# Expert visits ordered by early counts, gate and up columns split into even and odd, down tiles of the even rows first

## The reference

```
idx, gw = grouped_route(h, w_router, router_bias)      # 2 experts per token, weights sum to 1
order = argsort(idx.reshape(n_assign))                 # slots of one expert lie together
hb  = silu(xb @ w_gate[e]) * (xb @ w_up[e])            # 2048 -> 512
out = hb @ w_down[e]                                   # 512 -> 2048
y[token] += out * gw
x = x + g2 * y ;  return rms_norm(x, final_norm_w)
```

## Time and profile before

| | us |
|---|---|
| median of three runs | 2713.9 |
| profiled execution | 2711.68 |
| its span, first to last instruction | 2709.9 |
| TensorE busy | 2538.5 |
| first gate/up matmul of the expert loop | 1519.55 |
| last hidden transposes | 2681.22 |

### The profile page before, as it was taken

One profiled execution on the slowest core, in us unless ns is written; L12 is line 12 of the kernel. 1 busy time (PEld: TensorE's weight loads), 2 busy tenths in 40 slices (PEclk: granted clock), 3 DMA queues, 4 the chain that ended last, 5 costly groups with the idle time before them and its releaser, 6 DMA issues.

```text
span 2709.9 us, 30984 instructions
## 1 busy us (share of the span) xinstructions
PE 2538.5 (94%) x11966; PEld 1522.0 (56%) x11966; DVE 1302.8 (48%) x1559; ACT 640.4 (24%) x897; POOL 296.5 (11%) x505
## 2 busy tenths in 40 slices
PE   4999999999999987999998799999999898998897
PEld 3577888888768766777886333333333333333332
DVE  4379999999785777544334322222122121211124
ACT  4122222222212285323333111111111011110113
POOL 0000000000121111010001111111111111111111
PEclk8999999999999989999998899999999899999999
DMA  9933333333586572855636999899939999699997
GB/s 336 314 121 101 100 108 101 101 108 101 165 284 205 181 234 78 286 170 155 231 109 252 419 409 410 346 398 404 415 105 407 408 408 377 248 415 406 411 355 297
DMA packets 234063, 710.20 MB, mean 262 GB/s; under 512 B 26290, under 2 KB 120642, under 8 KB 186424
## 3 DMA queue, kind: packets, MB, share of 16 engines
q1 hardware_dynamic: 186624, 555.56, 53.0%
q0 software_dynamic: 37344, 125.58, 14.7%
q10 hardware_dynamic: 9998, 27.71, 2.8%
HBM read 657.60 MB, written 69.81 MB: 268 GB/s over the span
## 4 chain that ended last, share of the span: by engine, by line
PE 38%; DMA 19%; DVE 2%; issue 0%; ACT 0%; SPq 0%; POOL 0%; ACTq 0%; DVEq 0%; POOLq 0%
DMA ring<-in_w_down_dram 17%; PE ps L1739 16%; PE ps L1753 8%; PE ps L1961 4%; PE ps L1963 3%; PE ps L1962 3%; DMA wraw_o<-in_w_out_dram 2%; PE ps L1762 1%; PE ps L1679 1%; DVE tmp L2234 0%; PE ps L1771 0%; DVE hidT L2581 0%; DVE ring L2602 0%; DMA xrow<-h_d,tix 0%; PE ps L1976 0%
## 5 line engine op out<-in xcount | busy, mean ns | idle before, releaser
L1739 PE MATMUL ps<-ring,xT 128*64 128x512 f32 x3136 | 700.6, 604 | 39.6 <-DMA ring<-in_w_up_dram 38.2
L1739 PEld LDWEIGHTS ps<-ring,xT 128*64 128x64 f32 x3136 | 231.7, 139 | 500.7 <-issue 495.9
L1753 PE MATMUL ps<-ring,hidT 128*64 128x512 f32 x1568 | 348.8, 596 | 12.8 <-DMA ring<-in_w_down_dram 5.4
L2576 DVE TENSOR_TENSOR hb<-ps,gsl 128x256 f32<-128x256 f32 x49 | 20.8, 424 | 668.6 <-ACT gsl L2185 668.6
L763 PE MATMUL ps<-hh,wih 128*128 128x512 f32 x1056 | 330.7, 394 | 6.4 <-DVE wil L751 6.4
L763 PE MATMUL ps<-hh,wil 128*128 128x512 f32 x1056 | 331.2, 394 | 0.0
L763 PE MATMUL ps<-hl,wih 128*128 128x512 f32 x1056 | 329.4, 393 | 0.0
L1135 DVE SCALAR_TENSOR_TENSOR acc<-u,vcur,acc 128x1024 f32<-128x1024 f32 x240 | 308.2, 1284 | 7.8
L1753 PEld LDWEIGHTS ps<-ring,hidT 128*64 128x64 f32 x1568 | 107.6, 137 | 220.2 <-issue 191.3
L763 PEld LDWEIGHTS ps<-hh,wih 128*128 128x128 f32 x1056 | 198.9, 189 | 54.5 <-DVE wil L751 7.2
L763 PEld LDWEIGHTS ps<-hl,wih 128*128 128x128 f32 x1056 | 199.2, 189 | 44.4
(11 more groups left out here) (409 smaller groups left out, 3036.3 us busy)
## 6 DMA issues: line engine op xcount, KB each, us to landing
ring<-in_w_gate_dram SPq DMA_DIRECT2D x128, 1024.0 KB, 28.5
ring<-in_w_up_dram SPq DMA_DIRECT2D x128, 1024.0 KB, 30.6
ring<-in_w_down_dram SPq DMA_DIRECT2D x64, 2048.0 KB, 30.3
wm<-in_w_mod_dram POOLq DMA_DIRECT2D x88, 512.0 KB, 4.1
wraw_i<-in_w_in_dram SPq DMA_DIRECT2D x72, 512.0 KB, 3.8
wraw_o<-in_w_out_dram SPq DMA_DIRECT2D x128, 256.0 KB, 3.8
wmA<-in_w_mod_dram SPq DMA_DIRECT2D x32, 512.0 KB, 8.3
u<-in_w_mod_dram POOLq DMA_DIRECT2D x24, 512.0 KB, 4.7
```

The lines of the kernel that those rows point to most:

```text
L1739: last = pe.matmul(ps[BLK * a:BLK * a + BLK, BANK_GU:BANK_GU + FE], xT[:, t, h, :], ring[:, s:s + 2, c0:c0 + FE // 2], start=(q + k == 0), ...
L1753: last = pe.matmul(ps[BLK * a:BLK * a + BLK, BANK_D + 512 * n:BANK_D + 512 * n + 512], hidT[:, t, h, :], ring[:, slot(o, 8 + d), c0:c0 + 512],
```

## The change

Three things are changed.

1. `visit` is now a value that SP loads from DRAM for each expert. In the projection stage, VectorE counts how often the first 512 tokens chose each expert (a new TensorE matmul against ones at piece HALF + 54), ranks the experts (`rank_experts`), puts the ranks on the 32 places (`place_experts`) and stores the order. The router jobs of the first half move some pieces earlier for that. A place is 4 * step, plus 0 or 2 by bit 3 of the rank, plus 1 for the lower half, with step = (3 * (rank mod 8) + 3) mod 8. Block sums in visits order then come from products with two 32 x 32 matrices, `before` (visited earlier) and `at_visit`.
2. `gate_up` runs each quarter first for the even (r = 0) and then for the odd hidden columns (r = 1), with a column step of 2, into two PSUM banks. silu, product, transpose and copy are done per r, with a semaphore `s_gua` when the even ones are complete.
3. `down` takes the tiles 0, 2, 1, 3: both tiles of the even rows, then those of the odd rows.

```
-            def visit(o):
-                return o % G * EG + o // G
+            def visit(eng, o):
+                return eng.value_load(order_d[0:1, o:o + 1], min_val=0, max_val=E - 1)
...
-                        for k in range(4):
-                            h, t = k_tile(q, k)
-                            for a in range(2):
-                                c0 = FE * k + FE // 2 * a
-                                last = pe.matmul(ps[BLK * a:BLK * a + BLK, BANK_GU:BANK_GU + FE], xT[:, t, h, :],
-                                                 ring[:, s:s + 2, c0:c0 + FE // 2], start=(q + k == 0), stop=(q + k == 6))
+                        for r in range(2):
+                            for k in range(4):
+                                h, t = k_tile(q, k)
+                                for a in range(2):
+                                    c0 = FE * k + FE // 2 * a
+                                    last = pe.matmul(ps[BLK * a:BLK * a + BLK, BANK_GU[r]:BANK_GU[r] + FE // 2], xT[:, t, h, :],
+                                                     ring[:, s:s + 2, c0 + r:c0 + FE // 2:2], start=(q + k == 0), stop=(q + k == 6))
+                            if q == 3 and r == 0:
+                                last.then_inc(s_gua, 1)
                         last.then_inc(s_guq[q], 1)
...
-                    for d in range(FT):
-                        h, t = d // 2, d % 2
+                    for d in (0, 2, 1, 3):
+                        a_in, r = d // 2, d % 2
...
+                    sp.wait_ge(s_tab, 1)
+                    sp.dma_start(order_d[:, :], order_w[0:1, :]).then_inc(s_its, 16)
+                    sp.wait_ge(s_its, 16)
+                    experts = [visit(sp, o) for o in range(2)]
                     sp.wait_ge(s_wou, PIECES)
...
                     for r in range(NSLOT, NP * E):
+                        if r % NP == 0:
+                            expert = visit(sp, r // NP)
                         released(r - NSLOT)
...
+                        if g == HALF + 54:
+                            pe.wait_ge(s_ab, 1)
+                            pe.matmul(ps[:, BANK_EC:BANK_EC + HT * E], ones[:], oab[:].rearrange("p j e -> p (j e)"),
+                                      start=True, stop=True).then_inc(s_pre, 1)
...
                             gate_up(pe, j, o)
+                            transpose_hidden(pe, j, 0)
                             pe.wait_ge(s_xs, j + 2)
                             transpose_rows(pe, range(7))
-                            transpose_hidden(pe, j)
+                            transpose_hidden(pe, j, 1)
                             transpose_rows(pe, range(7, 8))
...
-                        act.wait_ge(s_guq[3], i + 1)
-                        act.activation(gsl[:], ps[:, BANK_GU:BANK_GU + FE // 2], ACT.Silu).then_inc(s_gs, 1)
+                        for r in range(2):
+                            act.wait_ge(s_gua if r == 0 else s_guq[3], i + 1)
+                            act.activation(gsl[:, P * r:P * r + P], ps[:, BANK_GU[r]:BANK_GU[r] + P], ACT.Silu).then_inc(s_gs, 1)
...
+                    def rank_experts():
+                        dve.wait_ge(s_pre, 1)
+                        red(ecnt[:], ps[:, BANK_EC:BANK_EC + HT * E].rearrange("p (j e) -> p e j", e=E), ALU.add)
+                        order(dve.scalar_tensor_tensor(out=key[:], in0=ecnt[:], scalar=float(2 * E), in1=wE[:], op0=ALU.mult, op1=ALU.add))
+                        tt(pairs[:], key[:, None, :].broadcast_to((P, E, E)), key[:, :, None].broadcast_to((P, E, E)), ALU.is_gt)
...
+                        if g == HALF + 57:
+                            rank_experts()
+                        if g == HALF + 58:
+                            place_experts()
...
-                    order(dve.tensor_copy(runs(nb[:]), visits(nb_i[:])))
-                    order(dve.tensor_tensor_scan(out=xinc[:], data0=ones[:, 0:E], data1=nb[:], initial=0.0,
-                                                 op0=ALU.mult, op1=ALU.add))
-                    tt(first[:], xinc[:], nb[:], ALU.subtract)
-                    ts(visits(code[:]), runs(first[:]), float(BLK), None, ALU.mult)
+                    ts(nb[:], nb_i[:], float(BLK), None, ALU.mult)
+                    dve.wait_ge(s_g2, 1)
+                    tt(sums[:], before[:], nb[:, None, :].broadcast_to((P, E, E)), ALU.mult)
+                    red(code[:], sums[:], ALU.add)
...
+                    tt(first[:], code[:], nb[:], ALU.add)
+                    tt(sums[:], at_visit[:], first[:, None, :].broadcast_to((P, E, E)), ALU.mult)
+                    red(xinc[:], sums[:], ALU.add)
+                    ts(xinc[:], xinc[:], 1.0 / BLK, None, ALU.mult)
```

More of the change, by code:

```diff
@@ L1480, in xt_piece @@
             def xt_piece(j):
[L1482 removed]
+                return HALF + 14 + 5 * j
             def landing(t):
@@ L1527, in slot, with load @@
                 return SLOT[(NP * o + m) % NSLOT]
-            def load(sp, o, m):
+            def load(sp, o, m, expert):
                 q, kind = m // 2, m % 2
+                e = ds(expert, 1)
                 s = slot(o, m)
@@ L1607, in hybrid_layer @@
             early = choice_tiles(0)
+            assert place_at[0] <= 68 * KB
+            place_at[0] = 68 * KB
+            oab = t3("oab", HT, E)
+            ecnt, key, rank = (t3(n, E) for n in ("ecnt", "key", "rank"))
+            rank_i, step_i = place("rank_i", [P, E], I32), place("step_i", [P, E], I32)
+            bits_i, bits = place("bits_i", [P, 2, E], I32), t3("bits", 2, E)
+            order_w = place("order_w", [P, E], I32)
             assert place_at[0] <= 72 * KB
+            at_visit, before = place("at_visit", [P, E, E], F32, 80 * KB), place("before", [P, E, E], F32, 84 * KB)
+            pairs, sums = place("pairs", [P, E, E], F32, 90 * KB), place("sums", [P, E, E], F32, 72 * KB)
             place_at[0] = xT_at
@@ L1764, in transpose_rows, with transpose_hidden @@
                             last.then_inc(s_xt2, 1)
-                def transpose_hidden(pe, j):
-                    pe.wait_ge(s_hb, j + 1)
-                    v = hb[:].rearrange("p (c t) -> p t c", t=2)
-                    for t in range(2):
-                        pe.transpose(ps[:, BANK_H + 512 * t:BANK_H + 512 * t + P], v[:, t, :], ident[:]).then_inc(s_hbt, 1)
+                def transpose_hidden(pe, j, r):
+                    pe.wait_ge(s_hb, 2 * j + r + 1)
+                    pe.transpose(ps[:, BANK_H + 512 * r:BANK_H + 512 * r + P], hb[:, P * r:P * r + P], ident[:]).then_inc(s_hbt, 1)
                 @block.sync
@@ L1812, in _ @@
                     for m in range(2, 6):
-                        load(sp, 1, m)
+                        load(sp, 1, m, experts[1])
                     sp.wait_ge(s_tbl, 1)
@@ L1816, in _ @@
                     for m in range(6, 9):
-                        load(sp, 1, m)
-                    sp.wait_ge(s_its, 16)
+                        load(sp, 1, m, experts[1])
+                    sp.wait_ge(s_its, 32)
                     n = item_before_last(sp)
@@ L1828, in released @@
                             sp.wait_ge(s_guq[m // 2], blocks_through(words, o))
+                    expert = experts[1]
                     for r in range(NSLOT, NP * E):
+                        if r % NP == 0:
+                            expert = visit(sp, r // NP)
                         released(r - NSLOT)
                         if r % NP < 8:
-                            load(sp, r // NP, r % NP)
+                            load(sp, r // NP, r % NP, expert)
                         elif r % 2 == 1:
-                            load(sp, r // NP, r % NP - 1)
+                            load(sp, r // NP, r % NP - 1, expert)
                     sp.wait_ge(s_dt[FT - 1], blocks_through(words, E - 2))
```

133 lines of the change are left out of this document (82 added, 51 removed).

## The result

The changed kernel took 2720.43 us (median of 8 runs, 2718.7 to 2725.48), the kernel before 2713.8 us beside it (8 runs, 2710.18 to 2715.53). The ratio is 1.0023, with a 95% interval of 1.0015 to 1.0032: 6.6 us slower by the medians, where 17 us faster was forecast and the range ended at 2718. The profiled execution took 2722.37 us, its span is 2720.6 us, 10.7 more than before's.

What follows compares the result with a forecast made beforehand. The expert loop was taken to alternate between TensorE and full DMA engines. Order -25, down +9, blocks -3, tables +3.7, counts +0.5 gave -15, taken as -17: 2697 us from 2713.9, range 2672 to 2718.

Steps and rivals of the forecast that it cites:

- the order with tables and counts: Expert loop: new visits order cuts stalls, -25 us; tables +3.7 before the first block; TensorE's count matmul +0.5.
- the two banks: Gate/up and hidden rows split in even and odd halves: net -0.2 us per block, -3 us over 14 blocks.
- the down order: Tiles 0, 2, 1, 3 need the last piece sooner and free tile 1's slot later: +9 us, range 0 to +14.
- the stall formula: Expert loop: TensorE's waits from weight pieces against blocks; with slow records, 64 us before and 39 after.
- Gate and up in two banks: Gate/up matmuls of 256 columns, step 2: +0.1 us per block from a fixed part per pair; the step free.
- The hidden rows: Between gate/up and down: even half's silu and product start earlier, transposes cover the odd half's; -0.3 us per block.
- The price of longer blocks: Expert loop: changes in block length are worth nothing where DMA sets the pace; counted in 14 blocks only.
- The tables: VectorE's added products and sums delay row indices and the first block: +3.7 us; projection stage nothing, up to 3.
- The further -2 us for fewer records at the low clock: Added to the sum: fewer waits leave fewer TensorE records at the low clock, taking -15 to -17.
- The weight loads: Gate/up: doubled loads of 0.14 us per pair stay hidden beside 0.2133 us of streaming.
- Rival 2: Expert loop: the order gives little, the late slot of tile 1 takes it; 2719 us, middle values 2712; 13%.
- Rival 1: Gate/up: short stepped matmuls don't stream; about 3320 us, open loads 3090, slightly open 2713 to 2735; together 14%.

Runs made afterwards that it cites:

- e1: Kernel before with only the new order of visits and its tables; gate/up, hidden rows and down tiles as before: 2704.3 us, ratio 0.9968.
- e11: Changed kernel with contiguous halves (no column step), w_down loaded to match in 8 KB pieces, down tiles in order: 2709 us, ratio 0.9982.
- e8: Changed kernel with the down tiles in order 0, 1, 2, 3 as before: 2714.1 us, ratio 0.9996.
- e3: Changed kernel with the last block's silu and product moved ahead of the squares and scaling of the first final rows: 2722.1 us, ratio 1.0034.
- e10: e1 with the first four final-row groups loaded earlier, into gate/up slots, and e3's move as well: 2704.7 us, ratio 0.9964.
- e4: Changed kernel with contiguous halves instead of even and odd columns (step 1; computes another function): 2714.9 us, ratio 1.0004.
- e7: Kernel before with its 512-column gate/up matmuls reading even, then odd columns (step 2): 2728.5 us, ratio 1.0048.

## Why the prediction was wrong, point by point

By the ratios, from before to after: the order with its tables -9 us (e1), two banks without the step +4 (e11 against e1), the step +4 (e8 against e11), the down order +7 (after against e8), each with an uncertainty of 3 to 4 us. They sum to +6 by construction. The two of +4 are hardly clear of nothing; the loads of w_down in smaller pieces are in both, with opposite signs. The second of the four has no cause shown: e11's blocks are shorter than e1's. Forecast were -21 for the order with tables and counts, -3 for the two banks and +9 for the down order. So the order missed by 12 us and the two banks by 11, and the sign of the whole needed both.

1. **The sum had no term for the end of the kernel.** This is the first of two failed steps. The order that the prediction lists ends in "2 1" and no longer in "1 2", and it used that only for the stall formula; what SP, ScalarE and VectorE do beside the last block was not read. The waits for weights did fall, by 26 us after and 32 in e1, about the -25 for the order. But TensorE's waits are the time only if TensorE ends last. Of e1's 32 us, 18.5 stand again in the last block, and e3 and e10 show that taking this idle away gives nothing back: the final rows, their squares and their scaling end last.
2. **"Gate and up in two banks": the term +0.1 us a block was mis-sized; it measured +0.78.** This is the second failed step. The fixed part per matmul, which the term was about, was right: +0.08 (e4). Missing was a term in columns: the step of 2 makes streaming 5% slower, at 256 columns and at 512 (e4, e7). The range of 13.81 to 14.8 us held the 14.61, for another reason than the one it was built on. The prediction said that it would be wrong above 14.2. The page "SBUF — State Buffer" of the Trainium skill, under its port tables, says that two hits in each 16-byte line give full speed. The traces don't agree: a step with two hits cost 0.70 us in 13.91.
3. **The hidden rows: right in kind, larger in size.** The middle part shrank by 0.50 us a block (1.78 to 1.28 by starts) where -0.3 was forecast.
4. **The price of longer blocks.** For the stretches where DMA sets the pace no cost was expected. That was right in part: 29 us of longer blocks cost 13 (e7). For gains it held more strongly: 33 us of shorter blocks gave 5.5 (e4 against after) and about 4 (e11 against e8).
5. **The down order: right in size.** +9 forecast from a range of 0 to 14; 12 us of waits and 7 us in the time (e8). Which of its two causes, the earlier need or the later slot, no run separates.
6. **The tables: right, a little too high.** +4.2 with the count matmul; from the last projection matmul to the first gate/up 2.3 us more (1469.60 to 1519.55, and 1473.01 to 1525.28). It is 49.5 to 50.3 us in the three profiles without the tables and 51.0 to 53.5 in the eleven with them. The projection stage cost nothing (387.2 and 387.1 us). The further -2 us for fewer records at the low clock counted something twice: the 64 and the 39 us held those records already.
7. **The weight loads: right.** Twice as many, and still beside the matmuls: 64 pairs take 13.91 us in e4, 0.2173 us a pair where streaming alone is 0.2133, which leaves no room for an open load of 0.14. The page "TensorE: Matmul & The Clock Gate" of the Trainium skill (What overlaps and what doesn't) says that a weight load overlaps running matmuls only where its row group differs. The traces don't agree: all loads here use the full 128 rows.
8. **The rivals.** Rival 2 (order -10, blocks -3, down +14, tables +4: 2719) came nearest in time, by luck: the formula's stalls came about as computed, 37.6 us for 39, and it was their gain that did not reach the end; the blocks were not shorter but longer. Rival 1 in its slight form (from 0.005 us a pair, 2713 to 2735) holds the measured time too, and its cost is there, 0.78 us in 64 pairs or 0.012 each, by the step and not by open weight loads. But it named no end of the kernel, and without the step the kernel is still no faster than before (e4, 1.0004).

## What to carry to other kernels

Where two engines are both near their limit (TensorE busy for 96 to 98%, the DMA engines for 93 to 94% of this loop), a sum over one engine's waits says how far that engine could go and not when the kernel ends: compute also the bytes over the full rate, and ask which of the two ends last. When the order of work changes, read what the other engines and queues do beside the last item, since its length may have been their cover. Two ways to cut a tile that are equal on paper need not be: price a strided operand by the column. The stride can move into a load (e11, with blocks of 22.11 us), which gained about 4 us here, hardly clear of nothing.

## What the runs showed that was not expected

- A moving operand with a step of two fp32 values streams 5% slower: 0.70 us in 13.91 for 64 pairs of 256 columns, 0.68 in 13.83 for 32 pairs of 512.
- 64 pairs of 256 columns take 13.91 us without a step, 32 pairs of 512 take 13.83: halving the width costs 0.6%.
- A load of 1 MB issued 8.0 us earlier into full DMA engines (405 and 424 GB/s) was ready 0.1 us earlier.
- Behind the idle of 18 us TensorE ran at the lower of its two levels: in the kernel after the granted clock was 0.50 from 2690.0 to 2692.3, and 0.89 over the last block's down tiles, which took 7.89 us; in e1 it was 0.76 over them and they took 9.25; 7.09 elsewhere.
